# Last layer's gate sums: spread over partitions by DMA instead of by matmuls, masks on GpSimd, the scores' extreme found in the pass that adds the bias

## The reference, cut to what matters

```python
# SSD mixer: 16 heads, chunks of 128 tokens; dt and a per head and token
a_cs = jnp.cumsum(dt5 * a.reshape(SSD_GROUPS, e), axis=2)
seg = at[..., :, None] - at[..., None, :]
decay = jnp.exp(jnp.where(tri, seg, -jnp.inf))
cb = jnp.einsum('bclgn,bcsgn->bcgls', cm, bm)
scores = cb[:, :, :, None] * decay
y_diag = jnp.einsum('bcgels,bcsgep->bclgep', scores, xdt)
# forgetting attention: 16 heads of 64, blocks of 128 queries with causal key prefixes
cum = jnp.cumsum(jax.nn.log_sigmoid(f_raw + f_bias), axis=1).transpose(0, 2, 1)
logits = jnp.einsum('bhqd,bhkd->bhqk', qh[:, :, start:end], kh[:, :, :end]) * scale
logits = logits + cum[:, :, start:end, None] - cum[:, :, None, :end]
p = jax.nn.softmax(jnp.where(causal, logits, -jnp.inf), axis=-1)
```

## Time and profile before

| | before |
|---|---|
| median of 3 runs | 1041.33 us (1041.1 to 1041.65) |
| profiled execution: time, span | 1041.01 us, 1039.2 us |
| TensorE busy | 1025.1 us, 99% |
| VectorE busy | 796.5 us, 77% |
| ScalarE busy | 635.4 us, 61% |
| GpSimd busy | 236.8 us, 23% |
| granted TensorE clock | 0.998 |

### The profile page before, as it was taken

How to read it: one execution, slowest core, us unless ns; L and a number is a source line. 1 busy time by engine, 2 the same in 40 slices (tenths; PEclk the granted TensorE clock), 3 DMA queues, 4 the chain that set the end, 5 groups by cost and what they waited for, 6 DMA issues and landing times.

```text
span 1039.2 us, 21815 instructions
## 1 busy us (share of the span) xinstructions
PE 1025.1 (99%) x7372; PEld 942.4 (91%) x7372; DVE 796.5 (77%) x1301; ACT 635.4 (61%) x1188; POOL 236.8 (23%) x204
## 2 busy tenths in 40 slices
PE   8999999999999999999999999999999999999998
PEld 7989988888889898888888899999898999999988
DVE  6875897877665988988777569978968579999853
ACT  7754775665554667766666456766666666666532
POOL 3200044444110000244443110000201034444300
PEclk9999999999999999999999999999999999999999
DMA  8543465655665332655666654543333355555563
GB/s 299 184 140 94 129 224 192 186 191 179 199 187 184 122 103 71 212 189 184 194 186 186 200 186 155 166 159 123 112 132 122 131 165 193 182 182 182 179 204 104
DMA packets 52483, 174.36 MB, mean 168 GB/s; under 512 B 5952, under 2 KB 7232, under 8 KB 52288
## 3 DMA queue, kind: packets, MB, share of 16 engines
q1 hardware_dynamic: 52416, 173.46, 52.1%
HBM read 172.39 MB, written 1.05 MB: 167 GB/s over the span
## 4 chain that ended last, share of the span: by engine, by line
PE 55%; DVE 5%; ACT 2%; issue 1%; DMA 0%; DVEq 0%; SPq 0%; ACTq 0%
PE bank L773 7%; PE bank L771 6%; PE bank L772 6%; PE scores L773 4%; PE scores L769 4%; PE scores L767 4%; PE bank L767 3%; PE bank L769 3%; PE scores L772 2%; PE scores L771 2%; PE scores L766 2%; PE bank L766 2%; PE bank L799 2%; PE bank L800 2%; PE bank L801 2%; DVE ring_parts L1735 1%
## 5 line engine op out<-in xcount | busy, mean ns | idle before, releaser
L1735 DVE TENSOR_TENSOR ring_parts<-ring_raw,ring_parts 128x1024 fp32r<-128x1024 f32 (+2 forms) x343 | 421.4, 1232 | 34.6 <-ACT ring_parts L1225 28.9
L1225 ACT ACTIVATE ring_parts<-ring_raw 128x1024 fp32r<-128x1024 f32 (+2 forms) x343 | 341.5, 999 | 63.2 <-PE scores L767 28.1
L773 PE MATMUL bank<-xw_parts,ring_parts 128*128 128x256 f32 x648 | 182.2, 281 | 0.0
L771 PE MATMUL bank<-xw_parts,ring_parts 128*128 128x256 f32 x472 | 136.6, 289 | 0.3 <-DVE con L1880 0.2
L772 PE MATMUL bank<-xw_parts,ring_parts 128*128 128x256 f32 x472 | 133.4, 283 | 0.0
L773 PEld LDWEIGHTS bank<-xw_parts,ring_parts 128*128 128x128 f32 x648 | 123.4, 190 | 7.5
L799 PE MATMUL bank<-ring_parts,xw_parts 128*128 128x256 f32 x384 | 112.9, 294 | 0.2 <-DVE u L1923 0.2
L800 PE MATMUL bank<-ring_parts,xw_parts 128*128 128x256 f32 x384 | 108.5, 283 | 0.0
L801 PE MATMUL bank<-ring_parts,xw_parts 128*128 128x256 f32 x384 | 108.4, 282 | 0.0
L773 PE MATMUL bank<-act_parts,ring_parts 128*128 128x256 f32 x381 | 107.8, 283 | 0.0
L1655 POOL TENSOR_TENSOR act_parts<-tmp,act_parts 128x256 f32 (+1 forms) x66 | 61.7, 935 | 166.3 <-ACT act_parts L1301 166.3
(11 more groups left out here) (273 smaller groups left out, 2555.0 us busy)
## 6 DMA issues: line engine op xcount, KB each, us to landing
ring_raw<-w_up SPq DMA_DIRECT2D x132, 512.0 KB, 3.6
ring_raw<-w_in SPq DMA_DIRECT2D x85, 512.0 KB, 3.6
ring_raw<-w_down SPq DMA_DIRECT2D x48, 512.0 KB, 3.5
ring_raw<-w_down SPq DMA_DIRECT2D x24, 384.0 KB, 4.0
ring_raw<-w_oa SPq DMA_DIRECT2D x16, 256.0 KB, 2.6
ring_raw<-w_ob SPq DMA_DIRECT2D x16, 256.0 KB, 2.9
ring_raw<-w_oa SPq DMA_DIRECT2D x8, 512.0 KB, 3.6
ring_raw<-w_ob SPq DMA_DIRECT2D x8, 512.0 KB, 3.6
```

Of the source, the lines that this page charges most:

```text
L771: mm(ps[:, 0:T], w_hi, high(parts, t), start=start, stop=False)
L773: return mm(ps[:, 0:T], w_lo, high(parts, t), start=False, stop=stop)
L1225: A(ring_hi[:, slot * DM:slot * DM + width], ring_raw[:, slot * DM:slot * DM + width], ACT.Copy).then_inc(hi_done, 1)
L1735: V.tensor_tensor(ring_lo[:, a:b], ring_raw[:, a:b], ring_hi[:, a:b].bitcast(f32), SUB).then_inc(lo_done, 1)
```

## The change

The running sums are stored to a DRAM tensor `small_rows` by two transfers on SyncE (slot 22 of its order). For each pair one more transfer loads two rows of it, repeated over all 128 partitions, 256 KB, into one of three SSD buffers or one of two attention buffers. The steps `ssd_decay` on TensorE and the two matmuls of each kind in `fox_scores` are gone, with `small_r`, `ident_r`, `mask_r` and `pick_r`.

SSD: GpSimd adds the token's own (negated) sum to the rows and clamps at 0 (`ssd_clamp`: four instructions per pair, slot a), ScalarE takes one exponential of 768 columns (slot a+1), and a is now 18 + 2p. In place of the mask, the diagonal blocks of C times B are multiplied once by a 0/1 matrix on VectorE (`cb_keep`, slot 15). The first group norm is at slot 29.

Attention: the queries' weight is negated, so that the scores come out with the other sign. GpSimd subtracts the mask matrix from the rows of the diagonal blocks (`fox_bias`, two instructions per pair, two slots ahead). VectorE adds scores and bias and keeps the minimum in four passes per pair, written to SBUF; ScalarE's exponentials read that.

```diff
@@ plans()
-    for s, slot in enumerate((13, 14, 14, 15)):
+    for s, slot in enumerate((13, 14, 14)):
         at(2, slot, "small", s)
+    at(2, 15, "cb_keep", 0)
...
     for p in range(8):
-        a = 17 + 2 * p
+        a = 18 + 2 * p
...
-        for n in range(2):
-            at(2, a + n, "ssd_decay", 2 * p + n)
+        at(2, a, "ssd_clamp", p)
+        at(2, a + 1, "ssd_decay", p)
...
+            at(2, slot - 2, "fox_bias", p)
             at(2, slot, "fox_scores", p)
...
-        plan[2][20 + 2 * p].insert(0, ("ssd_skip", p))
-    for g, slot in ((0, 28), (1, 40)):
+        plan[2][21 + 2 * p].insert(0, ("ssd_skip", p))
+    for g, slot in ((0, 29), (1, 40)):
@@ SyncE
+            def store_rows():
+                sp.wait_ge(dve_small, 7)
+                for n, row in enumerate((0, 64)):
+                    sp.dma_start(small_rows[16 * n:16 * n + 16, :], small[row:row + 16, 0:T]).then_inc(rows_stored, 16)
+            def load_rows(to, first, done):
+                sp.wait_ge(rows_stored, 32)
+                rows = small_rows[first:first + 2, :].partition_broadcast(P)
+                sp.dma_start(to, rows).then_inc(done, 16)
+            def load_ssd(p):
+                if p >= 3:
+                    sp.wait_ge(ss_y, p - 2)
+                load_rows(ssd_rows(p), 2 * p, ssd_loaded[p % 3])
+            def load_fox(p):
+                if p >= 2:
+                    sp.wait_ge(fx_m, 2 * (p - 2) + 2)
+                load_rows(fox_bias(p)[:, :, P:P + T], 16 + 2 * p, fox_loaded[p % 2])
+            SSD_LOADS = {23: (0, 1), 25: (2,), **{23 + 2 * p: (p,) for p in range(3, 8)}}
+            FOX_LOADS = {31 + 3 * p: p for p in range(8)}
@@ TensorE
             def fox_scores(layer, p):
...
-                for n in range(2):
-                    pick = pick_r[:, 16 + 2 * p + n:17 + 2 * p + n].to_broadcast([P, P])
-                    mm(bank[2 + n][:, 0:T + P], pick, small_r[:, 0:T + P], start=False, stop=False)
-                for n in range(2):
-                    mm(diagonals(bank[2 + n]), ident_r[:, :], both(mask_r), start=False, stop=True).then_inc(fx_s, 1)
...
-            def ssd_decay(layer, h):
...
-                mm(bank[7][:, 0:T + P], pick, small_r[:, P:2 * T], start=True, stop=False)
-                mm(diagonals(bank[7]), mask_r[:, :], both(ident_r), start=False, stop=True).then_inc(ss_bc, 1)
@@ ScalarE
+            def ssd_decay(layer, p):
+                act.wait_ge(ss_bc, 2 * p + 2)
+                A(ssd_pair(p), ssd_pair(p), ACT.Exp).then_inc(ss_e, 1)
@@ GpSimd
+            def ssd_clamp(layer, p):
+                pool.wait_ge(ssd_loaded[p % 3], 16 * (p // 3 + 1))
...
+                for h in heads_of:
+                    d = ssd_w(h)
+                    G.tensor_scalar(d[:, T:T + P], d[:, P:T], tok_neg[:, 16 + h:17 + h], 0.0, ADD, ALU.min).then_inc(ss_c, 1)
+                pool.wait_ge(ss_c, 2 * p + 2)
+                for h in heads_of:
+                    d = ssd_w(h)
+                    G.tensor_scalar(d[:, 0:T], d[:, 0:T], tok_neg[:, h:h + 1], 0.0, ADD, ALU.min).then_inc(ss_bc, 1)
+            def forget_bias(layer, p):
+                pool.wait_ge(fox_loaded[p % 2], 16 * (p // 2 + 1))
+                for n in range(2):
+                    b = fox_bias(p)[:, n, :]
+                    sums = b[:, P:3 * P].rearrange("p (t c) -> p t c", t=2)
+                    ends = b.rearrange("p (t c) -> p t c", t=3)[:, 0:3:2, :]
+                    last = G.tensor_tensor(ends, sums, cmat("causal").unsqueeze(1).to_broadcast([P, 2, P]), SUB)
+                last.then_inc(fx_b, 1)
@@ VectorE
+            def cb_keep(layer, _):
+                dve.wait_ge(cb_done, 2)
+                kept = cb.rearrange("p (g t c) -> p g t c", g=2, t=3)[:, :, 0:3:2, :]
+                V.tensor_tensor(kept, kept, cmat("keep").unsqueeze(1).unsqueeze(1).to_broadcast([P, 2, 2, P]),
+                                MUL).then_inc(cb_kept, 1)
...
             def fox_scores(layer, p):
-                dve.wait_ge(fx_s, 2 * p + 2)
-                for it, (a, width) in enumerate([(0, P), (P, T)]):
...
-                    last = V.tensor_reduce(negmax[:, it:4:2], both_heads, AX, ALU.max, negate=True)
-                last.then_inc(fx_m, 2)
+                dve.wait_ge(fx_b, p + 1)
+                if p:
+                    dve.wait_ge(fx_t, 2 * p)
+                for n in range(2):
+                    dve.wait_ge(fx_s, 2 * p + n + 1)
+                    s = fox_p(n)
+                    for it, (a, width) in enumerate([(0, P), (P, T)]):
+                        last = V.tensor_tensor_reduce(s[:, a:a + width], bank[2 + n][:, a:a + width],
+                                                      fox_bias(p)[:, n, a:a + width], 1.0, 3e38, ADD, ALU.min,
+                                                      negmax[:, 2 * n + it:2 * n + it + 1])
+                    last.then_inc(fx_m, 1)
```

More of the change, by code:

```diff
@@ L72 @@
 CONSTS = [("ident", 128), ("ones1024", 128), ("ones512", 128),
-          ("dist", 384), ("distT", 384), ("causal", 128), ("pick", 32), ("means64", 32), ("means128", 32), ("spread", 128), ("groups", 5)]
+          ("dist", 384), ("distT", 384), ("causal", 128), ("keep", 128), ("means64", 32), ("means128", 32), ("spread", 128), ("groups", 5)]
 CCOL, _at = {}, 0
@@ L108, in constants @@
     put("groups", np.concatenate([np.kron(np.eye(4), np.ones((32, 1))), low], 1))
-    put("pick", np.kron(np.diag([1, -1]), np.tile(np.eye(32)[:, :16], (2, 1))))
+    put("keep", (j >= i)[:P, :P])
     return c
@@ L341, in plans, with program @@
     return plan
-def program(nc, x_in, mem_in, params_in, consts_in, w, out):
+def program(nc, x_in, mem_in, params_in, consts_in, w, small_rows, out):
     f32, f32r = mybir.dt.float32, mybir.dt.float32r
@@ L422, in ssd_pair, with ssd_rows, fox_bias @@
         def ssd_pair(p):
-            room, a = (con, CCOL["dist"]) if p % 2 else (tmp, 1920)
+            room, a = ((tmp, 1920), (con, CCOL["dist"]), (u, 33 * T))[p % 3]
             return room[:, a:a + 768]
+        def ssd_rows(p):
+            return ssd_pair(p).rearrange("p (n c) -> p n c", n=2)[:, :, 0:T]
+        def fox_bias(p):
+            a = 36 * T + (p % 2) * 768
+            return u[:, a:a + 768].rearrange("p (n c) -> p n c", n=2)
         gate_s, gate, val, prod = (tmp[:, a:a + 512] for a in (0, 512, 1024, 1536))
@@ L476, in program @@
         exact = sem("exact")
+        rows_stored = sem("rows_stored")
+        ssd_loaded = [sem(f"ssd_loaded{n}") for n in range(3)]
+        fox_loaded = [sem(f"fox_loaded{n}") for n in range(2)]
+        fx_b = sem("fox_bias")
+        ss_c = sem("ssd_clamped")
         gs_sq, gs_sum = sem("group_sq"), sem("group_sum")
@@ L735, in _ @@
             load_kv(7)
+            def store_rows():
[16 more added lines that the diff above has]
+            FOX_LOADS = {31 + 3 * p: p for p in range(8)}
             for name, n, _, _ in PHASES:
                 ph = PH[name]
+                if name in ("in2", "oa2"):
+                    for c in range(n):
+                        slot = c + (PH["in2"].n if name == "oa2" else 0)
+                        if slot == 22:
+                            store_rows()
+                        load(ph, 0, c, n)
+                        for p in SSD_LOADS.get(slot, ()):
+                            load_ssd(p)
+                        if slot in FOX_LOADS:
+                            load_fox(FOX_LOADS[slot])
+                    continue
                 body = 12 if ph.per == 3 else 4
@@ L1044, in fox_scores @@
                     pe.wait_ge(fx_pt, 2 * p)
[L1045 to L1046 removed]
+                for it, a, width in ((0, 0, P), (1, P, T)):
                     for n in range(2):
                         r0 = 64 * n
[L1049 to L1055 removed]
+                        last = mm(bank[2 + n][:, a:a + width], u[r0:r0 + 64, q0 * T + it * P:q0 * T + (it + 1) * P],
+                                  u[r0:r0 + 64, k0 * T:k0 * T + width], start=True, stop=True)
+                        if it:
+                            last.then_inc(fx_s, 1)
             def fox_weights(layer, p):
@@ L1522, in fox_scores @@
                         c = 2 * n + it
-                        last = A(fox_p(n)[:, a:a + width], bank[2 + n][:, a:a + width], ACT.Exp,
-                                 bias=negmax[:, c:c + 1], accum_out=rowsum[:, c:c + 1])
+                        s = fox_p(n)[:, a:a + width]
+                        last = A(s, s, ACT.Exp, bias=negmax[:, c:c + 1], scale=-1.0, accum_out=rowsum[:, c:c + 1])
                     last.then_inc(fx_e, 1)
@@ L2351 @@
     ap = {n: nc.dram_tensor(n, list(m.shape), mybir.dt.float32, kind="ExternalInput").ap() for n, m in arrays.items()}
+    small_rows = nc.dram_tensor("small_rows", [32, T], mybir.dt.float32, kind="Internal").ap()
     out = nc.dram_tensor("out", [P, KT * T], mybir.dt.float32, kind="ExternalOutput").ap()
-    program(nc, ap["x_in"], ap["mem_in"], ap["params_in"], ap["consts_in"], {n: ap[f"w_{n}"] for n in w}, out)
```

(1 more changed line is left out.)

65 lines of the change are left out of this document (16 added, 49 removed).

## The result

The changed kernel takes 1046.22 us (median; 1045.57 to 1047.61) beside 1041.28 us before (1041.1 to 1041.65): ratio 1.005, 95% interval 1.0038 to 1.0062. It is slower by 5 us (0.5%), and no execution of the one overlaps those of the other. The forecast was faster, 1038.5 us, and the range up to 1043.8 does not hold the time.

A forecast was written before the change was run, and what follows sets the result against it. TensorE was taken to bound most stretches of 677 to 826 us, VectorE from 703.2, and a chain through VectorE and ScalarE 776.2 to 796.2. The terms summed to -2.8 us, giving 1038.5 us, range 1034.0 to 1043.8.

The forecast's parts named there:

- the sum without the clamps: SSD and attention parts, 677 to 826 us: every predicted change except the clamps' cost, -6.0 us.
- -6.0 + 4c: Whole change in us; c is VectorE's delay per SSD pair from GpSimd's clamps, taken as 0.8, ends 0 and 2.2.
- removed columns: TensorE, SSD and attention matmuls: 4.6 us saved in each, 9.3 us together, the most that can be won.
- score passes: Attention on VectorE: two maxima become four passes taking 1.10 us, +0.17 us per pair.
- step 2: 703.2 to 740.00 us, VectorE the bound: changes up to there together +1.2 us, of which clamps of four pairs +3.2.
- steps 4 to 6: From 751.8 us: two TensorE-bound stretches at -1.2 us each, and between them the chain of 776.2 to 796.2, +0.6.
- the price of the clamps: SSD: VectorE held up 0.37 us per 256-wide clamp, half per 128-wide, 1.1 per pair, times seven in ten, 0.8.
- The last sentence of the prediction: If GpSimd's clamps take over 1 us each while VectorE is elsewhere, their price was mis-sized.
- Rival C: Slots 24 to 34: GpSimd's instructions delay VectorE and become a late chain link; +4.5 us, 1045.8 us; chance 0.19.
- the load counted as 0: SyncE's queue: row loads are issued several slots before use, each at least 2.9 us, so they cost 0.
- the signs to look for: TensorE's idle in stretches three and five grows from 3.3 to 10 us or so; two-input VectorE instructions lengthen, 700 to 745.
- rival A: The whole 9.3 us saving arrives, VectorE's stretches shrinking as much as TensorE's: 1032.0 us; chance 0.10.

The follow-up runs named there:

- the mask sum with the earlier slot: Changed kernel with GpSimd adding a -1e30 mask once per pair in place of four clamps, load and GpSimd step one slot earlier: 1037.26 us, ratio 0.9961.

## Why the prediction was wrong

**Held in total, partly by luck: the sum without the clamps.** With the link out of the way the time is 1035.3 to 1036.1 us, 5 to 6 under before, as "-6.0 + 4c" gives it for c near 0 to 0.2. TensorE's busy time falls from 1025.1 to 1014.6 us in the version with the earlier clamps, no less than the 9.3 us of removed columns, and VectorE is the bound from 703 us on, once GpSimd is in time. But the halves are not as the sum had them. The attention's half alone gives -3.1 us, while its terms (score passes +0.3 and bias instructions +1.4 in step 2, -1.8 in steps 4 to 6) come to about 0. The state-space half is then worth only 2.1 us at its best (5.2 less 3.1), while most of the sum's 6 us lay there. The two errors offset each other.

**Right: the score passes.** Four passes run from 722.67 to the last read at 723.78 us, the 1.10 us of the earlier trace rows.

**Failed: the price of the clamps.** From the copy of the earlier trace rows, 0.48 us, I made a hold-up of VectorE of 0.37 us for each 256-wide one and half of that for a 128-wide one. The durations behind this are 0.48 and about 0.24 us, 1.4 us per pair, and no term of the sum had them. The rows of the changed kernel, two at a time where VectorE leaves them alone, and at their worst:

```profile
694.55 2.27 POOL L1729 TENSOR_SCALAR u<-u,tmp 128x256 f32<-128x256 f32 x2
723.37 1.41 POOL L1725 TENSOR_SCALAR u<-u,tmp 128x128 f32<-128x128 f32 x2
681.84 4.06 POOL L1725 TENSOR_SCALAR tmp<-tmp 128x128 f32<-128x128 f32 x2 [59.51 <-DMA tmp<-small_rows]
```

1.13 and 0.70 us each: 3.7 us per pair in place of 1.4, up to 6.3 where they meet VectorE. An addition and a minimum with a column operand took longer than the two-input add (0.73), which I had taken as the ceiling. The last sentence of the prediction named this case. The Trainium skill ("GPSIMD Engine Reference", Elementwise — side-by-side cycle accounting) gives about 1.8 cycles per element for a good one-input loop, 0.38 us as an estimate from that page; this form was three times slower here. The prediction set these 0.38 beside its own 0.37, but the one is a duration and the other was a hold-up.

**Failed: the kind of cost.** This is the step that failed. "GpSimd is idle enough. The cost is elsewhere" put c on VectorE only, and step 2 of the sum has the clamps as +3.2 us of VectorE's time and nothing for their own. GpSimd's time was on the chain itself: rows, clamps, exponential, weights, TensorE, and where ScalarE waited for it, TensorE stalled for 2.1, 2.9 and 3.4 us. Rival C named this place and the late link, but priced it as VectorE's delay and argued against it by what holds VectorE up. That its +4.5 lies near the measured +4.9 is luck: it is made of hold-ups of VectorE that the traces don't have. The range ended at 1043.8, short of rival C's own 1045.8, though it had a chance of 0.19.

**Failed: the load counted as 0.** "A load is issued several slots before its use": for pair 0 it is issued at 677.18 and lands at 681.75, and the first clamp waits for nothing else. At the second place (pair 4) and the last one (pair 7) the clamps wait for no load. Moving the loads a slot forward gave 4.2 us.

**Missing: the clock.** No step asked what a gap of TensorE does to what follows it. It is 2.9 us of the loss, without which the result would have been 1043.4: just inside the range, but still slower than before.

**Half right: the signs to look for.** TensorE's idle time did grow, in the four stretches shown from 2.0 to 10.4 us, but 6.4 of it lies in the first and the fourth, where I had TensorE as the bound; and ScalarE waits for the clamp. The long durations of two-input VectorE instructions did not come. Between 677 and 750 us the split of the weight tiles, before and after (count, busy us, mean ns, idle before):

```profile
L1735 DVE TENSOR_TENSOR ring_parts<-ring_raw,ring_parts 128x1024 fp32r<-128x1024 f32 x17 | 20.7, 1217 | 0.4 <-ACT ring_parts L1225 0.4
L1780 DVE TENSOR_TENSOR ring_parts<-ring_raw,ring_parts 128x1024 fp32r<-128x1024 f32 x17 | 21.2, 1247 | 0.8 <-ACT ring_parts L1257 0.8
```

Seventeen splits cost 0.5 us more, and the multiplication by C times B went down from a mean of 1.09 to 1.04 us over the eight pairs. By the prediction's own sign this meant a gain toward rival A; that sign, too, looked at VectorE only.

## What to carry to other kernels

When work moves to an idle engine, write down its latency in series first: load landing, every instruction at a duration measured for that very form, its place behind the others in that engine's order, and what waits at the end; idle share is no price. If the series has only a few microseconds to spare, move it a slot earlier in both the queue that loads and the engine that computes, here worth 10 us for two changed lines. A stall of TensorE as long as these should be priced with the clock behind it; here three of them cost 2.9 us on top.

## What the runs showed of the hardware

- GpSimd's add-and-minimum with a column operand: 1.13 us for 128x256, 0.70 for 128x128, against 0.73 for a two-input add of 128x256 and 0.48 for a copy.
- Between the two engines it was mostly GpSimd that got longer: two 128-wide clamps 1.41 us alone and up to 4.06 beside VectorE, the free-running add from 0.59 (1.18 for two) to 1.30, while VectorE's 1024-wide split, 1.22 us before, had means of 1.25 to 1.28. The Trainium skill ("SBUF — State Buffer", Who interferes with whom) calls the shared pair of ports an exclusive lock; the trace shows hold-ups of that kind, but here most of the waiting fell on GpSimd, of which the prediction had nothing.
- After stalls of 2.1, 2.9 and 3.4 us TensorE's granted clock went to 0.50 for about 3.4 us each time, 0.3 to 0.4 us after the work had begun again behind the first two. It isn't always so. In the execution profiled with the loads alone earlier the same stalls (2.87 and 3.45 us) had the clock at 0.50 for about 6.8 us each, from 716.6 and 750.8 on, while TensorE still stood; that execution was 2 us above its median, and the twice as long slow stretches may be why. A gap of 2.03 us in the version with the earlier clamps (it ended at 737.54) left the clock at 1.00, and one of 1.90 us in the mask sum with the earlier slot (it ended at 738.70) was followed by 0.50 for 3.4 us. So the length of the gap doesn't settle it; what does is left open.
- A broadcast load of two rows into 128 partitions (256 KB) landed 3.6 to 4.8 us after its issue (16 loads of the changed kernel, median 4.1), at a DMA share of 0.39 to 0.63 in the stretches shown.
